# Eight value slots, and the sample rows of a decoder step packed into two units of 128

## What is computed

```python
x  = x + g1 * (merged @ w_out)
h2 = rms_norm(x, norm2_w) * (1 + sc2) + sh2
...
s = einsum('thcd,hcnd->thcn', q, keys)          # 8 heads, 2 halves, 128 keys
sv, si = top_k(s, 16)
cv, ci = top_k(sv[:, :, 0, :, None] + sv[:, :, 1, None, :], 16)
idx = i1 * 128 + i2                             # 16 experts for each row and head
g = softmax(cv)
a = gelu(einsum('thkd,td->thk', expert_u[idx], h2))
y = einsum('thk,thkd->td', g * a, expert_v[idx])
x = x + g2 * y
```

## Time and profile before

| | us |
|---|---|
| median of 3 runs | 4593.65 |
| lowest and highest run | 4578.2, 5276.17 |
| the profiled execution's own time | 4595.73 |
| its span, first to last instruction | 4593.9 |

### The profile page before, as it was taken

One profiled execution on the slowest core, in us unless ns is written; L12 is line 12 of the kernel. 1 busy time (PEld: TensorE's weight loads), 2 busy tenths in 40 slices (PEclk: granted clock), 3 DMA queues, 4 the chain that ended last, 5 costly groups with the idle time before them and its releaser, 6 DMA issues.

```text
span 4593.9 us, 36647 instructions
## 1 busy us (share of the span) xinstructions
PE 2970.0 (65%) x11096; PEld 1311.4 (29%) x11096; DVE 2503.6 (54%) x6102; ACT 530.5 (12%) x1334; POOL 2451.6 (53%) x2238
## 2 busy tenths in 40 slices
PE   7779866778875577777666565455545545554556
PEld 1656754443521343333323221011111101110111
DVE  1143267775655556666555655555555555555551
ACT  0243112331001101222100000000000000000000
POOL 1000033335666666555565666666666667667773
PEclk9889977889986788888888786766666666666668
DMA  7422476669999999999999999999999999997776
GB/s 250 120 74 83 126 231 228 192 214 347 353 368 332 328 327 320 313 316 317 316 339 321 338 345 324 318 329 330 326 326 323 324 324 326 324 313 215 217 221 199
DMA packets 565767, 1290.41 MB, mean 281 GB/s; under 512 B 46986, under 2 KB 274634, under 8 KB 565498
## 3 DMA queue, kind: packets, MB, share of 16 engines
q0 software_dynamic: 305664, 1107.44, 68.7%
q1 hardware_dynamic: 233662, 149.33, 10.8%
q10 hardware_dynamic: 26246, 31.30, 2.1%
HBM read 1269.39 MB, written 20.55 MB: 281 GB/s over the span
## 4 chain that ended last, share of the span: by engine, by line
PE 34%; DMA 29%; POOL 17%; issue 9%; DVE 7%; ACT 2%; ACTq 0%; DVEq 0%; SPq 0%; POOLq 0%
DMA arena<-in_expert_v_dram,arena 26%; PE bank L1659 16%; POOL arena L552 9%; POOL arena L562 8%; PE bank L1479 8%; PE bank L1473 5%; DMA arena<-in_expert_u_dram,arena 2%; PE bank L1438 2%; DVE arena L1384 2%; PE bank L1516 1%; ACT arena L662 1%; PE bank L1496 1%; DVE arena L1038 0%; DVE arena L1043 0%; PE bank L1505 0%
## 5 line engine op out<-in xcount | busy, mean ns | idle before, releaser
L1659 PE MATMUL bank<-arena 128*32 128x512 f32 x4224 | 1511.9, 847 | 1342.7 <-DMA arena<-in_expert_v_dram,arena 1320.1
L1384 DVE CUSTOM_DVE_ANT_0 arena<-arena 128x1024 bf16<-128x1024 f32 (+1 forms) x1152 | 1401.8, 1225 | 1271.1 <-DMA arena<-in_expert_u_dram,arena 1105.7
L552 POOL DMA_INDIRECT arena<-in_expert_u_dram,arena x1152 | 1282.1, 1113 | 1067.7 <-DVEq L1303 515.5
L562 POOL DMA_INDIRECT arena<-in_expert_v_dram,arena x1056 | 1154.1, 1093 | 963.4 <-PE bank L1659 728.7
L1659 PEld LDWEIGHTS bank<-arena 128*32 128x32 f32 x4224 | 294.8, 135 | 2390.9 <-issue 2330.6
L1479 PE MATMUL bank<-arena 128*128 128x384 f32 (+1 forms) x2304 | 735.9, 476 | 5.9 <-DMA arena<-in_w_in_dram 4.2
L1479 PEld LDWEIGHTS bank<-arena 128*128 128x128 f32 x2304 | 447.5, 198 | 279.9 <-issue 63.4
L1473 PE MATMUL bank<-arena 128*128 128x128 f32 (+1 forms) x2880 | 344.5, 281 | 8.0 <-DVEq L1002 4.8
L1473 PEld LDWEIGHTS bank<-arena 128*128 128x128 f32 (+1 forms) x2880 | 333.3, 187 | 45.9 <-issue 33.1
L874 ACT COPY arena<-arena 128x4 f32<-128x4 f32 x264 | 52.4, 198 | 1774.7 <-PE bank L1659 1754.5
L1516 PE MATMUL bank<-arena 128*128 128x128 f32 x512 | 82.8, 313 | 50.9 <-ACTq L685 37.6
(11 more groups left out here) (178 smaller groups left out, 1608.3 us busy)
## 6 DMA issues: line engine op xcount, KB each, us to landing
arena<-in_w_in_dram SPq DMA_DIRECT2D x156, 512.0 KB, 5.0
arena<-in_w_ada_dram SPq DMA_DIRECT2D x12, 2048.0 KB, 8.0
arena<-in_expert_u_dram,arena POOLq DMA_INDIRECT x1152, 6.1
arena<-in_expert_v_dram,arena POOLq DMA_INDIRECT x1056, 5.9
arena<-in_w_out_dram SPq DMA_DIRECT2D x24, 512.0 KB, 7.2
arena<-in_w_query_dram SPq DMA_DIRECT2D x24, 512.0 KB, 6.5
arena<-in_x_prompt_dram SPq DMA_DIRECT2D x16, 512.0 KB, 8.2
x_d<-arena ACTq DMA_DIRECT2D x8, 512.0 KB, 5.8
```

What stands on the lines that cost most here:

```text
L552: pool.indirect_dma_start(out=u_ring[u % RING][0:p, :], out_offset=None, in_=eu, in_offset=bass.IndirectOffsetOnAxis(ap=at_k, axis=0)).the ...
L562: pool.indirect_dma_start(out=v_ring[v % RING][:, :], out_offset=None, in_=ev, in_offset=bass.IndirectOffsetOnAxis(ap=idxT[tau % 2][:, t:t ...
L1384: V.tensor_tensor_reduce(out=prod[u % 2][0:p, :], in0=u_ring[u % RING][0:p, :], in1=hE[tau % 2][0:p, :], scale=1.0, scalar=0.0, op0=ALU.mu ...
L1659: last = M(banks(c, 1)[32 * q:32 * q + 32, :], w_mid[x // 4 % 2][:, x % 4, 31 - j:63 - j], v_ring[x % RING][:, 512 * c:512 * c + 512], sta ...
```

## The change

1. The v ring has eight slots (`VRING`) instead of four; `add_tokens` takes two tokens at a time as before. Room comes from `y_tmp`, whose part the h2 buffers `hE` take over, and from G1, A2 and B2.
2. The sample is 2 units instead of 8: unit 64 holds heads 0 to 3 and unit 65 heads 4 to 7, with head q of the four in partitions 32q to 32q + 31. Its h2 is loaded four times, its query columns four side by side, and its scores come from four matmuls into the four quadrants. To turn indices and weights into columns by token, `by_head` spreads 128 x 32 values over 128 columns with zeros outside the row's own head (`sel_q`), and a matmul with `sel_s` (four 32 x 32 identities) sums them. The loop runs over `PERIODS` = 74 steps of 16, with u in the first 66.
3. G1, A2 and B2 are loaded in each group's output stage into `mc`: SP waits for the group's last merge and issues the three loads between the weights of output blocks 3 and 4. DVE waits for them at block 0. norm2_w is folded into the modulation before it is stored (9 rows). G2 stays in a buffer of its own.

```diff
-UNITS = ETILES * PH
+UNITS = NT * PH + 2
+PERIODS = PH + UNITS
+HEADS = [PH] * NT + [2]
-RING = 4
+RING, VRING = 4, 8
...
+        sel_s, sel_q = carve(NS), carve(4)
         mc = carve(KC, J * P)
+        G1, A2, B2 = (at(mc_at + i * D, D) for i in range(3))
-        v_ring = [carve(D) for _ in range(RING)]
+        v_ring = [carve(D) for _ in range(VRING)]
-        y_tmp = carve(D)
...
                 for b in range(WRING, BLOCKS):
                     weights(g, b)
+                    if b == QB + CB + AB + 3:
+                        sp.wait_ge(mg_made, 8 * (g + 1))
+                        sp.dma_start(G1[:, :], mod_p[:, 2 * D:3 * D].to_broadcast([P, D])).then_inc(rows_in, 16)
+                        sp.dma_start(A2[:, :], mod_p[:, 4 * D:5 * D].to_broadcast([P, D])).then_inc(rows_in, 16)
+                        sp.dma_start(B2[:, :], mod_p[:, 3 * D:4 * D].to_broadcast([P, D])).then_inc(rows_in, 16)
...
-                if v >= RING:
-                    pool.wait_ge(v_free, v - RING + 1)
+                if v >= VRING:
+                    pool.wait_ge(v_free, v - VRING + 1)
...
-            for n in range(UNITS + NS // TOPK):
+            for n in range(PERIODS):
...
             def load_h2(tau):
+                if tau >= 3:
+                    act.wait_ge(y_made, tau - 2)
+                if tau == NT:
+                    for q in range(4):
+                        act.dma_start(hE[0][NS * q:NS * q + NS, :], h2_d[NT, 0:NS, :]).then_inc(h2_in[0], 16)
...
             def out_rows(g, b):
                 if b == 0:
                     dve.wait_ge(xo_in, 16 * J * (g + 1))
+                    dve.wait_ge(rows_in, 16 * 7 + 48 * (g + 1))
...
+            def by_head(out, values):
+                link(V.tensor_tensor(out.rearrange("p (u q k) -> p u q k", u=2, q=4),
+                                     values.unsqueeze(2).to_broadcast([P, 2, 4, TOPK]),
+                                     sel_q[:, :].unsqueeze(1).unsqueeze(3).to_broadcast([P, 2, 4, TOPK]), ALU.mult))
...
             def key_scores(n):
+                if n >= NT * PH:
+                    for q in range(4):
+                        last = M(E_PS[NS * q:NS * q + NS, 0:2 * PK], q_st[n % 2][:, NS * q:NS * q + NS],
+                                 keys_bd[:, 4 * (n % PH) + q, :], start=True, stop=True)
```

More of the change, by code:

```diff
@@ L95, with ends_tile @@
 RING_AT = ring_entries()
+def ends_tile(n):
+    return n == UNITS - 1 or n < NT * PH and n % PH == PH - 1
 def single_entries():
     keys = [("s", 0)]
-    for n in range(UNITS):
-        tau, h = n // PH, n % PH
-        if h == 0 and tau:
-            keys.append(("w", tau - 1))
+    for n in range(PERIODS):
+        if n % PH == 0 and n:
+            keys.append(("w", n // PH - 1))
         if n + 1 < UNITS:
             keys.append(("s", n + 1))
-        if h == PH - 1:
-            keys.append(("x", tau))
-    keys.append(("w", NT))
+        if ends_tile(n):
+            keys.append(("x", n // PH))
     return {key: i for i, key in enumerate(keys)}
@@ L228, in build @@
         maskt = carve(3, 2, P)
+        u_sb_at = cursor[0]
         u_sb = carve(J * P)
@@ L283, in build @@
         kcT = carve(NKV, NB * WIN + NS)
-        G1s, A2s, B2s, n2s = (at(e_at + i * D, D) for i in range(4))
+        G1s, A2s, B2s = (at(e_at + i * D, D) for i in range(3))
         cv_sb = carve(NB, KVW)
@@ L359, in build @@
         u_in = [sem(f"u_in_{r}") for r in range(RING)]
-        v_in = [sem(f"v_in_{r}") for r in range(RING)]
+        v_in = [sem(f"v_in_{r}") for r in range(VRING)]
         q_in = [sem(f"q_in_{r}") for r in range(2)]
@@ L877, in exp_gates @@
             def exp_gates(tau):
-                p = PARTS[tau]
+                every = gate[:, 0:HEADS[tau], :].rearrange("p h k -> p (h k)")
                 act.wait_ge(gsub_made, tau + 1)
-                link(A(gate[0:p, :, :].rearrange("p h k -> p (h k)"), gate[0:p, :, :].rearrange("p h k -> p (h k)"), ACT.Exp))
+                link(A(every, every, ACT.Exp))
                 act.sem_inc(gexp_made, 1)
@@ L919, in _ @@
                         keep_scores(n + 1)
+                    if n == NT * PH and k == 6:
+                        load_g2_sample()
                     if h == PH - 1 and k == 4 and tau:
@@ L925, in _ @@
                         load_query(n + 2)
-                    if h == PH - 1 and k == 14:
+                    if ends_tile(n) and k == 14:
                         exp_gates(tau)
@@ L933, in _ @@
                     raise AssertionError("steps left")
-            activate(NT)
-            keep_wT(NT)
-            store_y(NT - 1)
             load_x2(NT)
-            for b in range(1, NS // 4):
-                place_w(NT * P // 4 + b)
             store_y(NT)
@@ L962, in _ @@
                 cols = slice(n * ABLK, (n + 1) * ABLK)
-                V.tensor_tensor(mod9[0:NB + 1, cols], banks(n % ARING, 1)[0:NB + 1, :], bada9[0:NB + 1, cols],
-                                ALU.add).then_inc(ada_free, 1)
+                link(V.tensor_tensor(mod9[0:NB + 1, cols], banks(n % ARING, 1)[0:NB + 1, :], bada9[0:NB + 1, cols], ALU.add))
+                if n == 9:
+                    sc2 = mod9[0:NB + 1, 4 * D:5 * D]
+                    link(V.scalar_tensor_tensor(out=sc2, in0=sc2, scalar=1.0, in1=n2_9[0:NB + 1, :], op0=ALU.add, op1=ALU.mult))
+                dve.sem_inc(ada_free, 1)
             dve.wait_ge(modT_ps, 1)
@@ L1684, in _ @@
                         key_scores(n + 1)
-                    if h == PH - 1 and k == 5:
+                    if ends_tile(n) and k == 5:
                         turn_index(tau)
@@ L1691, in _ @@
                     raise AssertionError("steps left")
-            turn_w(NT)
-            for t in range(0, NS, 2):
-                add_tokens(NT * P + t)
 _INS = ['x_prompt', 'x_sample', 'cache_k', 'cache_v', 'state_conv', 'c_prompt', 'c_sample',
```

228 lines of the change are left out of this document (117 added, 111 removed).

## The result

The changed kernel takes 4068.67 us (median of four runs, 4055.78 to 4072.52) where the kernel before takes 4592.36 (median of four beside it): a ratio of 0.886, 95% interval 0.883 to 0.890. The forecast was 4283 us with a range down to 4180; the direction was right, and the gain, 524 us, is two thirds larger than the 313 us of the sum and outside the range. The profiled execution took 4055.78 us with a span of 4054.0 us, the fastest of the four; against the profile of before (4593.9 us) it is 539.9 us shorter, and all that follows is read from these two.

What follows compares the result with a forecast made beforehand. The v ring of four was taken to bound the middle, and POOL's count of gathers units 64 to 71. Savings of 7 + 44 + 90 + 152 + 20 = 313 us gave 4596 - 313 = 4283 us, range 4180 to 4445.

Steps and rivals of the forecast that it cites:

- The loop through a ring of four: Units 38 to 63: the four-slot v ring sets the pace, 16 tokens needing 50 us against 52.5 per unit.
- the last stretch: The sample's own 32 tokens at the end: 72 us against 92, 20 saved.
- The stage with the packed sample: From unit 64, sample rows as two units of 128: 242 us against 394, 152 saved.
- the price of a unit behind the ring: Units 38 to 63 with eight v slots: 49 us a unit, set by DMA share, 90 us saved.
- Units 16 to 37: Eight v slots beside the fronts: 2 us a unit, 44 us saved, bounds 0 and 102.
- Units 8 to 15: Eight v slots at a DMA share of 0.97: 7 us saved, bounds 0 and 14.
- The rows and the start: Output rows loaded per group, and selector memsets and small load at the start: hidden, 0 us.
- A: Rival: the middle gains nothing, POOL or the DMA engines being full already; 4441 us, chance 0.17.
- B: Rival: the DMA engines reach share 1.00 everywhere; 399 us saved, 4197 us, chance 0.15.
- C: Rival: TensorE stays at 1.2 GHz in the last stages; 4370 us, chance 0.08.
- D: Rival: slower, up to eight v in flight lowering the DMA rate in units 8 to 63; 4895 us, chance 0.02.
- E: Rival: A and C together, no change seen at the end of the path; 4518 us, chance 0.03.

Runs made afterwards that it cites:

- half rows: The changed kernel gathering rows of 2 KB in place of 4 KB, with products and matmuls of the same size: 4009.7 us (one run).
- half products: The changed kernel with DVE's product over 512 columns in place of 1024: 3831.51 us (one run).
- six u slots: The changed kernel with the same twelve slots split six for u and six for v: 4051.37 us, 0.882 of before.

## Why the prediction was too small

**What it had right.** The loop through a ring of four was what held the middle: cutting the ring back brought all of it back. POOL's wait for PE went, the share rose above 0.96, TensorE was granted 0.97 of its clock with v alone (the 2.4 GHz level), and pairs of the sample follow at 3.44 us (16 in 55.1 us from 3993.62). That TensorE would get the full level in the stretch with v alone came right by luck: the reason given was that it had it where PE was the busiest, but in the earlier trace rows PE was busier in units 8 to 15 (337.92 of 455 us, granted 0.85) than in the last stretch (63.80 of 92, granted 0.94). The stage with the packed sample (179 us against 152) and the last stretch (23 against 20) were near.

**The step that failed** is the price of a unit behind the ring: "share 0.92 raised to 1.00 is 354 GB/s and 48.3 us", and the 49 taken between it and 49.8. It read the busy share of the DMA engines as a scale on which the rate rises in proportion to a ceiling. It is none: at shares of 0.98 to 1.02 the same engines moved 366, 371, 402 and 407 GB/s, and half the bytes showed not half the share but 0.64. The trace had 372 in the earlier trace rows; the prediction used it as an outer bound only. What came next behind the ring was not the transfers but POOL, which the prediction had priced at 43.4 us a unit and then passed over, 48.3 being the larger. Its price had to be read with the collisions of the earlier trace rows at the new density: 43.4 became (1181 us / 26) 45.4, and the units 46.0. The term was 167 us, not 90. That 46.0 is also the far end of the bounds is chance: the bound came from the rate of 372 GB/s, and with POOL unhindered the same transfers went on to 402. The Trainium skill (DMA: Bandwidth & Descriptors, "Where 436 GB/s comes from") has a core's HBM traffic bound near 358 GB/s, which it works out as the half of a stack that two cores share. This kernel runs on one core, and its transfers ran at 402 to 407, so the measurement decides.

**Units 16 to 37** failed in the same step, and in a second: 139 us against 44, above its own bound of 102. The bound was the share again. And the reason for taking less than half of it, that DVE's waits inside the fronts cure by no slot, looked at DVE; POOL's waits in that stage, 315.4 us for PE, were not looked up. Of these 308 went, 132 came back at the u slots, and the gathers, their issue and the lists took 37 more: 139 are left. Units 8 to 15 (28 against 7) fell short by the share too.

**The stage from unit 64.** With v alone a token costs 1.3 us, near POOL's 1.24, not the 1.48 that 354 GB/s gave. The ordinary units 64 and 65 took 44.9 and 44.8 us instead of 49.

**The rows and the start.** Taken as 0. Of the waits of 25 us, 9.9 lie in group 0, where PE goes on without a pause (its weight loads start at 490.58, 496.21 and 501.84), so there they were hidden as forecast; 8.1 and 7.0 lie in groups 1 and 2, for which the prediction had named 12 and 6. What they are worth is not settled (22 us by the medians). The start got 4 us shorter; with the ring of four (605.0) and with the packing undone (604.2) it did too, so neither of the two makes it; why was not tried.

**The rivals.** A fell with the first window after: POOL's collisions are real, but 46 us is far from 52.5, and of the rule named for it only one side shows: products lengthen gathers, and no gather lengthens a product. B was nearest, at 4197, and too slow for the same reason as the forecast: its ceiling of 354. C, D and E did not occur: the clock was 0.97 with v alone, and the rates rose.

**Open.** What holds units 16 to 37 now at 51.8 us: half rows took them to 49.2, half products to 48.6, six u slots to 50.9, so no one edit accounts for it.

## What to carry to other kernels

Before pricing what a longer ring frees, write down the account of the engine that issues the transfers, stage by stage: its own work, its issue, and its waits by name. It must add up to the stage, and the wait that goes is the most that can be gained, less the wait that is late next. A DMA share near 1 does not say how fast the transfers can go: here it stood at 0.98 to 1.02 from 366 to 407 GB/s. The best steady stretch of a trace is a lower bound of the ceiling; here it was 372, and the transfers went to 407. Where the issuing engine is the bound, look at what lengthens its instructions: here moving one operand of another engine's product into PSUM was worth 100 us, and two parts of a change that meet at one bound were worth more together than the sum of each alone.

## What the runs showed of the hardware that was not expected

- A gather issued by POOL that begins inside a DVE product with two operands in SBUF takes up to the rest of the product longer (0.94 us free, 1.97 in the rows shown), and inside one with an operand in PSUM it does not (945 ns on the mean, with as many products as long). The product is not lengthened the other way: 308 of 383 in units 40 to 63 of the kernel after begin while a gather runs, and none of these takes over 1.25 us.
- What the collisions cost depends on where in the product a gather begins: with half the bytes as many gathers met a product (385 of 768), but earlier in it, and the units got slower, 48.0 against 46.0 us, with v gathers at 1403 ns on the mean and u gathers at 986.
- Gathers of 128 rows of 4 KB ran at 402 and 403 GB/s over stretches of a thousand us, at 407 with v alone; the DMA share shown was then 1.02, and 0.64 at 181 GB/s with rows of 2 KB.
